# Five RMS norms around the end of the output projection: more of the squares' sum on VectorE, less on TensorE

## The chip, the cores and the metric

One core of one Trainium2 chip runs the whole kernel. The metric is the device time of one execution in microseconds (us), taken as the median of the runs. Engine names as in the profile: PE is TensorE (matmuls), PEld its weight load, DVE is VectorE, ACT is ScalarE, POOL is GpSimd, SP is the engine that issues the DMA transfers.

## The reference, cut to what matters

One layer of a decoder trunk, 1024 prompt tokens and 8 sample tokens, width 1024, all in fp32:

```python
def rms_norm(x, g):
    xf = x.astype(jnp.float32)
    r = xf * lax.rsqrt(jnp.mean(xf * xf, axis=-1, keepdims=True) + EPS)
    return (r * g.astype(jnp.float32)).astype(x.dtype)

def half_step_ffn(x, g_pre, g_post, w_gu, w_down):
    h = rms_norm(x, g_pre)
    gate, up = jnp.split(h @ w_gu, 2, axis=-1)
    y = (jax.nn.silu(gate) * up) @ w_down
    return x + 0.5 * rms_norm(y, g_post)

# per layer
xp = half_step_ffn(xp, ...)                                  # first FFN
att, ho = attention(...), hgrn2(...)                         # mixer
xp = xp + rms_norm(mixer_output(att, ho, ...), mix_post_g)   # output projection (1024 x 1024), its norm, the residual
xp = half_step_ffn(xp, ...)                                  # second FFN, with its own norm ahead
```

The change concerns the norm behind the output projection (`mix_post_g`) and the norm ahead of the second FFN: for each token the mean of 1024 squares.

## The kernel before

Activations lie with the 1024 features on partitions: 8 tiles (`KT`) of 128 features, and the 1032 tokens in three groups g of 344 (`GW`). So each activation of a group is 128 x 8 x 344. To keep fp32 accuracy, every dense product is split: ACT makes a rounded copy of weights and activations (`w_hi`, `x_hi`, type fp32r), DVE makes what is left (`w_lo`, `x_lo`, by a subtraction), and PE multiplies hi by hi, lo by hi and hi by lo. A unit is one output tile of one group: 8 x 3 matmuls of 344 columns.

**A norm.** ACT squares the group into one of two buffers (`square`: `sq_a` or `sq_b`, 8 tiles). DVE adds the upper half to the lower half (`fold`: 8 tiles become 4). PE multiplies what is left by a matrix of ones into one PSUM bank, and so sums over partitions and tiles at once (`norm_sum`; these matmuls are plain fp32, not the split kind, and the trace holds two records for each, so that x8 is four of them). ACT takes logarithm and exponential of it (`inverse`), which gives the reciprocal root `rms` or `rms_y`. A norm is named ("F", 1, g) where it belongs to the output projection's result y, and ("S", 2, g) where it belongs to the residual stream ahead of the second FFN. For eight other norms, named in `folded_twice`, DVE already adds a second time (4 tiles become 2) and PE has two tiles to sum. ("F", 1, 2) is done in halves by functions of its own (`last_fold`, `last_sum`) and is not touched.

**The order of the work.** Nothing is scheduled at run time: each engine has its instructions in an order written out by hand, and waits on semaphores. Around the change:

- PE: 24 output projection units k = 0..23 (`out_units`), group g = k // 8. The sums stand between them: ("F",1,0) behind unit 12, ("F",1,1) behind unit 18, ("S",2,0) behind unit 19. Then the halves of ("F",1,2), and between them and behind them the first units of the second FFN (`pair_unit`, by group and number o = 0 or 1: (0,0), (0,1), then ("S",2,1), then (1,0), (1,1), (2,0), then ("S",2,2), then (2,1)). Then `ffn`: six more opening units and the pair loop.
- DVE: for each unit k, `out_split(k)` (`w_lo` of the unit's weights) and `out_evac(k)` (PSUM to y). Among them stand the folds; `scaled(g)` (y times the reciprocal root), `added(g)` (y times gain, plus residual), `border_low(g)` (`x_lo` of the second FFN's input); and for group 2, behind the fold of ("S",2,1), `last_new` (the same scaling and adding in halves), `last_low`, and the fold of ("S",2,2). Behind that: `open_gate` and `open_up` (evictions of the FFN's first units), `normed`, and the sums and splits that the pair loop of the FFN needs.
- ACT: `out_split(k)` (`w_hi`), `square_y(g)`, `inverse`, `border_hi(g)` (`x_hi` for the second FFN from the new residual; waits for `added(g)`), `square_x(g)`.

The DVE part in the order written out, from the fold of ("F",1,1) on (set here on fewer lines):

```python
            fold(("F", 1, 1))
            out_split(19); out_evac(17); out_split(20)
            border_fold(0)
            out_evac(18); scaled(1); out_split(21); out_evac(19)
            added(1)
            out_split(22); out_evac(20); last_fold(0)
            out_split(23); out_evac(21); split_lo(G_FFN2, 0)
            border_low(1)
            out_evac(22); split_lo(G_FFN2 + 1, 1); out_evac(23)
            last_fold(1)
            border_fold(1)
```

ACT makes `w_hi` of unit 23 behind `border_hi(1)`, and `border_hi(1)` waits for `added(1)`. `Seq` (called `seq`) makes DVE wait for the end of its own instruction before the next.

Of the kernel before, what the change touches and what calls it, by code (L numbers as in the profile page):

```python
# [11 lines left out]
ALU = mybir.AluOpType  # L12
# [9 lines left out]
KT = D_MODEL // P  # L22
# [158 lines left out]
def build(nc, ins, outs):  # L181
    ctx = ExitStack()
    with ctx:
# [10 lines left out]
        def put(name, shape, dt, offset=None):  # L194
            size = (2 if dt == BF16 else 4) * int(np.prod(shape[1:]))
            if offset is None:
                offset = at[0]
                at[0] += (size + 31) // 32 * 32
            assert offset + size <= end, (name, offset + size - end)
            return nc.alloc_sbuf_tensor_at(name, shape, dt, offset=offset)  # L200
# [25 lines left out]
        sq_bufs = [put("sq_a", [P, KT, GW], F32), put("sq_b", [P, KT, GW], F32, h_at + 4 * GW * 4)]  # L226
# [68 lines left out]
        F, KG, HI, v_raw, HG = (FK[:, 0], FK[:, 3]), (FK[:, 1], FK[:, 4]), FK[:, 2], FK[:, 4], FK[:, 0:4]  # L295
# [54 lines left out]
        S = sems  # L350
# [6 lines left out]
        norm_no = {n: i for i, n in enumerate(norms)}  # L357
        sq_no = {n: 1 if n in (("S", 0, 1), ("F", 0, 1), ("S", 1, 1), ("S", 1, 0), ("S", 2, 0), ("S", 2, 1), ("S", 2, 2), ("F", 2, 1)) else 0 for n in norms}
        fold_no = {n: k for k, n in enumerate(n for n in norms if n[0] == "S")}
        y_fold_no = {n: k for k, n in enumerate(n for n in norms if n[0] == "F" and n[2] != (2 if n[1] == 1 else 0))}  # L360
# [4 lines left out]
        LAST_S1 = norm_no[("S", 1, 0)] + 1  # L365


        folded_twice = (("S", 0, 1), ("S", 0, 2), ("F", 0, 2), ("F", 0, 1), ("S", 1, 2), ("S", 1, 1), ("F", 2, 2), ("F", 2, 1))

        GAIN_F = {0: half_gain[:, 0, :], 1: vecs[:, V_GAIN["mix_post"]:V_GAIN["mix_post"] + 8], 2: half_gain[:, 1, :]}  # L370

# [246 lines left out]
        def _(pe):  # L618
# [13 lines left out]
            def norm_sum(n):  # L632
                i = norm_no[n]
                if n in fold_no:
                    pe.wait_ge(S["sq_folded"], fold_no[n] + 1)
                elif n in y_fold_no:
                    pe.wait_ge(S["y_folded"], y_fold_no[n] + 1)
                else:
                    pe.wait_ge(S["sq_done"], i + 1)
                tiles = KT // 4 if n in folded_twice else KT // 2 if n in fold_no or n in y_fold_no else KT  # L640
                if i >= 2:
                    pe.wait_ge(S["root_done"], i - 1)
                for m in range(tiles):
                    mm = nc.tensor.matmul(PS[:, sum_bank[n], :GW], ones[:], sq_bufs[sq_no[n]][:, m, :],  # L644
                                          start=(m == 0), stop=(m == tiles - 1))
                mm.then_inc(S["ss_done"], 1)

            def ffn(n0, u0, f, b):
# [118 lines left out]
                for k in range(BLOCKS):  # L767
                    block(k)
                    if k == 75:
                        norm_sum(("F", b, 2))  # L770
                    if k == 88:
                        norm_sum(("F", b, 1))
                    if b == 0 and k == 108:
                        pe.wait_ge(S["d_copied"], COPIED * f + N_LEAD)
                        norm_sum(("S", 1, 2))
                    if b == 0 and k == 116:
                        norm_sum(("S", 1, 1))
                    if k == 118:
                        half_sum(b, 0)
# [1031 lines left out]
        def _(dve):  # L1811
            seq = Seq(dve, S["dve_seq"])
# [10 lines left out]
                nc.vector.tensor_tensor(w_lo[s][:], raw[s][:], w_hi[s][:].bitcast(F32), ALU.subtract)\  # L1823
                    .then_inc(S["w_ready"], 1)

            def fold_again(n):

                q = sq_bufs[sq_no[n]]
                seq(nc.vector.tensor_tensor(q[:, 0:KT // 2], q[:, 0:KT // 2], q[:, KT // 2:], ALU.add))
                nc.vector.tensor_tensor(q[:, 0:KT // 4], q[:, 0:KT // 4], q[:, KT // 4:KT // 2], ALU.add)\  # L1830
                    .then_inc(S["y_folded" if n[0] == "F" else "sq_folded"], 1)

            def fold(n):
                if n in folded_twice:
                    dve.wait_ge(S["sq_done"], norm_no[n] + 1)
                    fold_again(n)
                    return
                q = sq_bufs[sq_no[n]]
                dve.wait_ge(S["sq_done"], norm_no[n] + 1)
                nc.vector.tensor_tensor(q[:, 0:KT // 2], q[:, 0:KT // 2], q[:, KT // 2:], ALU.add)\  # L1840
                    .then_inc(S["y_folded" if n[0] == "F" else "sq_folded"], 1)

            half_of = lambda a: slice(KT // 2 * a, KT // 2 * (a + 1))
# [53 lines left out]
            def ffn(n0, u0, f, b, slot_uses, hooks={}):  # L1897
# [272 lines left out]
                def fold_lead():  # L2170
# [3 lines left out]

                two = lambda a, b: lambda: (a(), b())
                behind = {2: lambda: h_sums(PAIR_STEPS, 1), 3: lambda: down_sums(PAIR_STEPS), 13: u2, 24: v, 30: c22, 35: c12, 37: lambda: fold(("F", b, 2)),
                          40: c21, 41: lambda: scaled_half(b, 2, 0), 42: lambda: scaled_half(b, 2, 1), 43: lambda: added_half(b, 2, 0),
                          44: lambda: fold(("F", b, 1)), 45: lambda: added_half(b, 2, 1),
                          49: lambda: scaled_half(b, 1, 0), 50: lambda: scaled_half(b, 1, 1), 51: lambda: added_half(b, 1, 0), 52: lambda: added_half(b, 1, 1),
                          59: fold_lead}  # L2180
                if b == 0:
                    behind.update({46: lambda: low_half(b, 2, 0, None), 47: lambda: low_half(b, 2, 1, S["x_split_lo"]),
                                   53: lambda: fold(("S", 1, 2)),
                                   54: lambda: low_half(b, 1, 0, None), 55: lambda: low_half(b, 1, 1, S["x_split_lo"]),
                                   57: lambda: fold(("S", 1, 1))})
# [390 lines left out]
                gained_low(1, g)  # L2576

            def border_fold(g):
                n = ("S", 2, g)
                q = sq_bufs[sq_no[n]]  # L2580
                dve.wait_ge(S["sq_done"], norm_no[n] + 1)
                nc.vector.tensor_tensor(q[:, 0:KT // 2], q[:, 0:KT // 2], q[:, KT // 2:], ALU.add).then_inc(S["sq_folded"], 1)

            def last_fold(a):
                q = sq_bufs[sq_no[("F", 1, 2)]]
# [107 lines left out]
            out_evac(17)  # L2693
            out_split(20)
            border_fold(0)
            out_evac(18)
            scaled(1)
# [12 lines left out]
            out_evac(23)  # L2710
            last_fold(1)
            border_fold(1)

            def last_halves():
# [3 lines left out]
            def last_lows():  # L2718
                last_low(0)
                last_low(1)  # L2720
                border_fold(2)
# [97 lines left out]
```

## Time and profile before

| | us |
|---|---|
| median of 3 runs | 1896.4 (1896.36 to 1897.34) |
| the profiled execution, its own time | 1896.69 |
| its span in the trace | 1894.9 |
| PE busy | 1869.7 (99% of the span) |
| DVE busy | 1369.5 (72%) |
| ACT busy | 802.9 (42%) |

The span is 1.8 us shorter than the execution's own time; that lies around it. Matmuls are pipelined and their ends are modelled: one of 344 columns is shown with 0.32 us and the next starts 0.16 us behind it. So a PE that is busy in the table need not be at its peak, and the starts of its instructions say more than its busy time. The same holds in part for DVE, whose instruction may start before the one ahead has ended.

### The profile page before, as it was taken

The numbers are of one execution on the slowest core, as the hardware profiler recorded it, in microseconds if no ns is written. First come the engines' busy times: TensorE is split into PE (matmuls) and PEld (weight loads), VectorE is DVE, ScalarE is ACT, GpSimd is POOL, SyncE is SP. The second block draws the span as 40 slices with busy tenths as digits, with TensorE's granted clock in tenths as the row PEclk, the third lists the DMA queues.
The fourth block names the chain that finished last, engine by engine and source line by source line (L and its number), as shares of the span: only waits on it lengthen the run. The fifth ranks groups of instructions, "written<-read, shape, count | busy, mean of one in ns | idle before, by whom it ended". The sixth has DMA issues, their size and how long they took to land. (4 is left out here: it accounts for less than half of the span.)

```text
span 1894.9 us, 36314 instructions
## 1 busy us (share of the span) xinstructions
PE 1869.7 (99%) x14337; PEld 1825.7 (96%) x14337; DVE 1369.5 (72%) x2127; ACT 802.9 (42%) x1278; POOL 35.0 (2%) x27
## 2 busy tenths in 40 slices
PE   9999999999999999999999999999999999999997
PEld 8999999999999999998998899999999999999997
DVE  7866767766656885578888678976776667755784
ACT  6422222323455673146565646532232223354553
POOL 0000000000000000000001100000000000000000
PEclk9999999999999999999999999999999999999999
DMA  5243334344798783210101465243334433599775
GB/s 190 101 160 130 138 132 144 122 155 159 257 294 262 221 264 117 56 49 25 36 25 35 141 242 171 83 158 136 144 122 152 150 138 132 172 310 292 226 240 181
DMA packets 115307, 296.60 MB, mean 157 GB/s; under 512 B 13136, under 2 KB 44760, under 8 KB 110328
## 3 DMA queue, kind: packets, MB, share of 16 engines
q1 hardware_dynamic: 115048, 294.93, 45.9%
q8 instruction: 84, 1.38, 0.3%
q14 instruction: 31, 0.25, 0.0%
q10 hardware_dynamic: 144, 0.03, 0.0%
HBM read 221.25 MB, written 73.00 MB: 155 GB/s over the span
## 5 line engine op out<-in xcount | busy, mean ns | idle before, releaser
L759 PE MATMUL PS<-x_hi,w_hi 128*128 128x344 f32 x960 | 309.3, 322 | 3.6 <-DVE w_lo L2122 3.6
L761 PE MATMUL PS<-x_hi,w_lo 128*128 128x344 f32 x960 | 306.7, 319 | 0.0
L760 PE MATMUL PS<-x_lo,w_hi 128*128 128x344 f32 x960 | 306.3, 319 | 0.0
L1290 ACT ACTIVATE silu_g<-silu_g 128x344 f32<-128x344 f32 x92 | 44.9, 491 | 458.8 <-DVE silu_g L2100 254.5
L663 PE MATMUL PS<-x_hi,w_hi 128*128 128x344 f32 x640 | 204.5, 320 | 0.0
L664 PE MATMUL PS<-x_lo,w_hi 128*128 128x344 f32 x640 | 204.1, 319 | 0.0
L665 PE MATMUL PS<-x_hi,w_lo 128*128 128x344 f32 x640 | 203.7, 318 | 0.0
L2129 DVE TENSOR_TENSOR x_lo<-t_raw,x_hi 128x688 fp32r<-128x688 f32 x120 | 104.1, 867 | 114.0 <-ACT x_hi L1398 113.4
L759 PEld LDWEIGHTS PS<-x_hi,w_hi 128*128 128x128 f32 x960 | 180.3, 188 | 5.6 <-DVE w_lo L2122 4.7
L760 PEld LDWEIGHTS PS<-x_lo,w_hi 128*128 128x128 f32 x960 | 180.2, 188 | 0.8
L761 PEld LDWEIGHTS PS<-x_hi,w_lo 128*128 128x128 f32 x960 | 180.2, 188 | 0.0
L1398 ACT ACTIVATE x_hi<-t_raw 128x688 fp32r<-128x688 f32 x120 | 92.8, 773 | 188.6 <-DMA t_raw<-spill_h 188.5
L1979 DVE TENSOR_TENSOR s_lo<-s_raw,s_hi 128x512 fp32r<-128x512 f32 x160 | 106.9, 689 | 82.0 <-ACT s_hi L1316 82.0
L1316 ACT ACTIVATE s_hi<-s_raw 128x512 fp32r<-128x512 f32 x160 | 100.5, 630 | 146.5 <-DVE s_raw L2086 138.8
L654 PE MATMUL PS<-x_sum,s_hi 128*128 128x344 f32 x480 | 154.1, 321 | 5.3 <-DVE s_lo L1979 4.9
L2122 DVE TENSOR_TENSOR w_lo<-raw,w_hi 128x1024 fp32r<-128x1024 f32 x120 | 146.9, 1224 | 14.0 <-ACT w_hi L1387 8.6
L654 PE MATMUL PS<-x_hi,w_hi 128*128 128x344 f32 x480 | 153.5, 320 | 0.9 <-ACT rms L1349 0.9
L655 PE MATMUL PS<-x_sum,s_hi 128*128 128x344 f32 x480 | 153.8, 320 | 0.0
L656 PE MATMUL PS<-x_sum,s_lo 128*128 128x344 f32 x480 | 153.7, 320 | 0.0
L656 PE MATMUL PS<-x_hi,w_lo 128*128 128x344 f32 x480 | 153.1, 319 | 0.0
L655 PE MATMUL PS<-x_lo,w_hi 128*128 128x344 f32 x480 | 152.7, 318 | 0.0
L1823 DVE TENSOR_TENSOR w_lo<-raw,w_hi 128x1024 fp32r<-128x1024 f32 x111 | 135.4, 1220 | 11.9 <-ACT w_hi L1253 7.0
(311 smaller groups left out, 4436.2 us busy)
## 6 DMA issues: line engine op xcount, KB each, us to landing
raw<-in_w_gu SPq DMA_DIRECT2D x88, 512.0 KB, 4.2
t_raw<-spill_h SPq DMA_DIRECT2D x238, 172.0 KB, 2.8
raw<-in_w_down SPq DMA_DIRECT2D x152, 256.0 KB, 3.6
d_raw<-in_w_down SPq DMA_DIRECT2D x44, 512.0 KB, 6.2
spill_s<-d_sum SPq DMA_DIRECT2D x22, 1024.0 KB, 5.2
raw<-spill_s SPq DMA_DIRECT2D x88, 256.0 KB, 4.4
spill_h<-T SPq DMA_DIRECT2D x22, 688.0 KB, 3.1
spill_h<-h_odd SPq DMA_DIRECT2D x22, 516.0 KB, 2.7
```

What stands on the lines that cost most here:

```text
L654: nc.tensor.matmul(PS[:, bank, :GW], wh[:, c], vh[:, k], start=(start and k == 0), stop=False, skip_group_check=not start)
L655: nc.tensor.matmul(PS[:, bank, :GW], wh[:, c], vl[:, k], start=False, stop=False, skip_group_check=not start)
L656: mm = nc.tensor.matmul(PS[:, bank, :GW], wl[:, c], vh[:, k], start=False, stop=(k == KT // 2 - 1), skip_group_check=not start)
L663: nc.tensor.matmul(PS[:, 7, :GW], wh, vh, start=(k == 0), stop=False)
L664: nc.tensor.matmul(PS[:, 7, :GW], wh, vl, start=False, stop=False)
L665: mm = nc.tensor.matmul(PS[:, 7, :GW], wl, vh, start=False, stop=(k == KT - 1))
L759: nc.tensor.matmul(PS[:, bank, :GW], hi[:, c], vh, start=opens, stop=False, skip_group_check=again)
L760: nc.tensor.matmul(PS[:, bank, :GW], hi[:, c], vl, start=False, stop=False, skip_group_check=again)
L761: mm = nc.tensor.matmul(PS[:, bank, :GW], lo[:, c], vh, start=False, stop=closes, skip_group_check=again)
L1823: nc.vector.tensor_tensor(w_lo[s][:], raw[s][:], w_hi[s][:].bitcast(F32), ALU.subtract)\
L1979: nc.vector.tensor_tensor(s_lo[k][:], s_raw[k][:], s_hi[k][:].bitcast(F32), ALU.subtract).then_inc(S["s_low"], 1)
L2122: return nc.vector.tensor_tensor(to[:], src[:], hi[:].bitcast(F32), ALU.subtract)
```

## The change

The choice of how often a norm's squares are added on DVE becomes a table. The norms ("S",0,0) and ("S",1,0) stay at one addition, the eight of the list stay at two. Five change: ("F",1,0), ("F",1,1) and ("S",2,2) get two additions instead of one (PE sums 2 tiles instead of 4), and ("S",2,0) and ("S",2,1) get three (PE sums 1 tile instead of 4).

```diff
-        folded_twice = (("S", 0, 1), ("S", 0, 2), ("F", 0, 2), ("F", 0, 1), ("S", 1, 2), ("S", 1, 1), ("F", 2, 2), ("F", 2, 1))
+        folds = {n: 1 for n in (*fold_no, *y_fold_no)}
+        folds.update({n: 2 for n in (("S", 0, 1), ("S", 0, 2), ("F", 0, 2), ("F", 0, 1), ("S", 1, 2), ("S", 1, 1), ("F", 2, 2), ("F", 2, 1))})
+        folds.update({("F", 1, 0): 2, ("F", 1, 1): 2, ("S", 2, 0): 3, ("S", 2, 1): 3, ("S", 2, 2): 2})
...
-                tiles = KT // 4 if n in folded_twice else KT // 2 if n in fold_no or n in y_fold_no else KT
+                tiles = KT >> folds.get(n, 0)
...
             def fold(n):
-                if n in folded_twice:
-                    dve.wait_ge(S["sq_done"], norm_no[n] + 1)
-                    fold_again(n)
-                    return
                 q = sq_bufs[sq_no[n]]
                 dve.wait_ge(S["sq_done"], norm_no[n] + 1)
-                nc.vector.tensor_tensor(q[:, 0:KT // 2], q[:, 0:KT // 2], q[:, KT // 2:], ALU.add)\
+                w = KT // 2
+                for _ in range(folds[n] - 1):
+                    seq(nc.vector.tensor_tensor(q[:, 0:w], q[:, 0:w], q[:, w:2 * w], ALU.add))
+                    w //= 2
+                nc.vector.tensor_tensor(q[:, 0:w], q[:, 0:w], q[:, w:2 * w], ALU.add)\
                     .then_inc(S["y_folded" if n[0] == "F" else "sq_folded"], 1)
...
             def border_fold(g):
-                n = ("S", 2, g)
-                q = sq_bufs[sq_no[n]]
-                dve.wait_ge(S["sq_done"], norm_no[n] + 1)
-                nc.vector.tensor_tensor(q[:, 0:KT // 2], q[:, 0:KT // 2], q[:, KT // 2:], ALU.add).then_inc(S["sq_folded"], 1)
+                fold(("S", 2, g))
```

## Rows read from the trace of the kernel before

**Rows 1.** The page: busy time by engine, share of the span, instructions.

```profile
PE 1869.7 (99%) x14337; PEld 1825.7 (96%) x14337; DVE 1369.5 (72%) x2127; ACT 802.9 (42%) x1278; POOL 35.0 (2%) x27
```

**Rows 2.** Busy time by stretch: length, PE, PEld, DVE, ACT, POOL, clock, DMA.

```profile
1150.00:1175.00 25.00, 25.00 (x148) 23.41 (x147) 22.37 (x29) 13.97 (x20) 0.00 (x0) 1.00 0.37 110
...
1205.00:1245.00 40.00, 39.52 (x250) 38.84 (x248) 37.98 (x50) 18.04 (x35) 0.00 (x0) 1.00 0.15 43
```

**Rows 3.** Timeline of PE around the sum of ("F",1,1): start, duration, instruction.

```profile
1153.22 0.32 PE L1075 MATMUL PS<-x_hi,w_lo 128*128 128x344 f32 x1
1153.37 2.48 PE L644 MATMUL PS<-sq_a,ones 128*128 128x344 f32 x8
...
1155.84 0.32 PE L1074 MATMUL PS<-x_lo,w_hi 128*128 128x344 f32 x1
```

**Rows 4.** Timeline of DVE: a fold and what follows; three small operations.

```profile
1150.72 1.58 DVE L1840 TENSOR_TENSOR sq_a<-sq_a 128x1376 f32<-128x1376 f32 x1
1152.22 1.22 DVE L2556 TENSOR_TENSOR w_lo<-raw,w_hi 128x1024 fp32r<-128x1024 f32 x1
...
1235.78 0.51 DVE L1987 TENSOR_TENSOR T<-h_even 128x344 f32<-128x344 f32 x1
1236.33 0.52 DVE L1991 TENSOR_TENSOR T<-h_odd,T 128x344 f32<-128x344 f32 x1
1236.76 0.51 DVE L1992 TENSOR_TENSOR T<-h_odd,h_even 128x344 f32<-128x344 f32 x1
```

**Rows 5.** One source line: second addition of the norms that have two.

```profile
L1830 DVE TENSOR_TENSOR sq_b<-sq_b x4: 874/875/877, 24.3 to 1814.2; 128x688 f32<-128x688 f32 x4
```

**Rows 6.** Timeline around the sum of ("F",1,0); in brackets idle time and releaser.

```profile
1126.03 1.58 DVE L1840 TENSOR_TENSOR sq_a<-sq_a 128x1376 f32<-128x1376 f32 x1
...
1128.23 2.47 PE L644 MATMUL PS<-sq_a,ones 128*128 128x344 f32 x8
...
1130.74 0.55 ACT L1268 ACTIVATE root<-PS,eps 128x344 f32<-128x344 f32 x1 [4.94 <-PE PS L644]
...
1131.85 3.02 DVE L2565 TENSOR_TENSOR y<-y,rms_y 128x2752 f32<-128x2752 f32 x1 [2.68 <-ACT rms_y L1273]
```

**Rows 7.** Timeline of DVE, ACT and PE from unit 18's eviction to unit 23.

```profile
1156.42 0.51 DVE L2560 COPY y<-PS 128x344 f32<-128x344 f32 x1
...
1156.98 3.02 DVE L2565 TENSOR_TENSOR y<-y,rms_y 128x2752 f32<-128x2752 f32 x1
...
1161.49 3.98 DVE L2571 SCALAR_TENSOR_TENSOR resid<-y,vecs,resid 128x344 f32<-128x344 f32 x8
...
1165.51 3.90 ACT L1278 ACTIVATE x_hi<-resid,vecs 128x344 fp32r<-128x344 f32 x8 [0.29 <-DVE resid L2571]
...
1169.31 1.04 ACT L1700 ACTIVATE w_hi<-raw 128x1024 fp32r<-128x1024 f32 x1
...
1170.38 1.22 DVE L2556 TENSOR_TENSOR w_lo<-raw,w_hi 128x1024 fp32r<-128x1024 f32 x1 [2.57 <-ACT w_hi L1700]
...
1173.05 0.32 PE L1073 MATMUL PS<-x_hi,w_hi 128*128 128x344 f32 x1
```

**Rows 8.** Timeline of DVE and PE, the border to the second FFN.

```profile
1182.86 1.59 DVE L2582 TENSOR_TENSOR sq_b<-sq_b 128x1376 f32<-128x1376 f32 x1 [1.52 <-ACT sq_b L1259]
...
1192.38 3.98 DVE L2612 SCALAR_TENSOR_TENSOR x_lo<-resid,vecs,x_hi 128x344 fp32r<-128x344 f32 x8
...
1197.46 1.59 DVE L2582 TENSOR_TENSOR sq_b<-sq_b 128x1376 f32<-128x1376 f32 x1 [1.10 <-ACT sq_b L1259]
...
1200.25 2.47 PE L644 MATMUL PS<-sq_b,ones 128*128 128x344 f32 x8
```

**Rows 9.** Timeline of DVE and PE, opening of the second FFN to its first pair.

```profile
1206.52 0.52 DVE L1922 TENSOR_TENSOR h_even<-PS,rms 128x344 f32<-128x344 f32 x1 [1.16 <-PE PS L807]
...
1245.55 0.69 DVE L1979 TENSOR_TENSOR s_lo<-s_raw,s_hi 128x512 fp32r<-128x512 f32 x1 [0.70 <-ACT s_hi L1316]
...
1246.50 0.40 PE L654 MATMUL PS<-x_sum,s_hi 128*128 128x344 f32 x1 [1.53 <-DVE s_lo L1979]
```

More of the change, by code:

```diff
@@ L1824, in split_lo @@
                     .then_inc(S["w_ready"], 1)
-            def fold_again(n):
-                q = sq_bufs[sq_no[n]]
-                seq(nc.vector.tensor_tensor(q[:, 0:KT // 2], q[:, 0:KT // 2], q[:, KT // 2:], ALU.add))
-                nc.vector.tensor_tensor(q[:, 0:KT // 4], q[:, 0:KT // 4], q[:, KT // 4:KT // 2], ALU.add)\
-                    .then_inc(S["y_folded" if n[0] == "F" else "sq_folded"], 1)
             def fold(n):
-                if n in folded_twice:
-                    dve.wait_ge(S["sq_done"], norm_no[n] + 1)
-                    fold_again(n)
-                    return
                 q = sq_bufs[sq_no[n]]
                 dve.wait_ge(S["sq_done"], norm_no[n] + 1)
-                nc.vector.tensor_tensor(q[:, 0:KT // 2], q[:, 0:KT // 2], q[:, KT // 2:], ALU.add)\
+                w = KT // 2
[3 more added lines that the diff above has]
+                nc.vector.tensor_tensor(q[:, 0:w], q[:, 0:w], q[:, w:2 * w], ALU.add)\
                     .then_inc(S["y_folded" if n[0] == "F" else "sq_folded"], 1)
@@ L2578, in border_fold @@
             def border_fold(g):
-                n = ("S", 2, g)
-                q = sq_bufs[sq_no[n]]
-                dve.wait_ge(S["sq_done"], norm_no[n] + 1)
-                nc.vector.tensor_tensor(q[:, 0:KT // 2], q[:, 0:KT // 2], q[:, KT // 2:], ALU.add).then_inc(S["sq_folded"], 1)
+                fold(("S", 2, g))
             def last_fold(a):
```

## The prediction, made before the run

> **What bounds the kernel now.** The page says PE: 99% busy, DVE 72% [rows 1]. That is a mean over stages, so I read next the busy time by stretch around the change. PE is busy throughout, but DVE is at 22.37 of 25 us around the last output units and at 37.98 of 40 us in the opening of the second FFN [rows 2]. Two engines are full there at once, and what the change takes from one it gives to the other. So the question is not how much PE saves, but which of the two each wait of the other ends at. For that I read the timelines of PE, DVE and ACT side by side [rows 6 to 9]: the reader is to look for the places where DVE stands idle (there it has slack) and for the releaser in brackets.
>
> **What PE saves.** Matmuls of a unit start 0.157 us apart. The last one ahead of the sum of four tiles starts at 1153.22, and the second one behind it at 1155.84; without the sum it would have started at 1153.22 + 2 x 0.157 = 1153.53. So four tiles cost 2.31 us, one tile 0.577 [rows 3]. The change removes 2 + 2 + 3 + 3 + 2 = 12 tiles: 6.92 us of PE.
>
> **What DVE pays.** A single fold occupies the queue for 1.50 us (1150.72 to 1152.22, though its own duration is 1.58: the next one overlaps the end). An operation that must wait for the one ahead starts 0.04 behind its end: 0.55 us from start to start for one of 0.51, against 0.43 where nothing is waited for [rows 4]. So with a second addition: 1.58 + 0.04, then 0.875 for 128x688 [rows 5] less the overlap of 0.08, together 2.41: **+0.91 us**. With a third: 1.62 + 0.91 + 0.43 = 2.96: **+1.46 us**; the add of one tile is not in the trace as a fold, I take 0.51 from the 128x344 adds [rows 4]. Over the five: 3 x 0.91 + 2 x 1.46 = 5.65 us. No DMA, and nothing on ACT or POOL, is added or moved.
>
> The trace shows 0.12 us more between two small operations where the second waits for the first [rows 4]. The Trainium skill (VectorE: DVE Perf Modes, section "The DRAIN you can't avoid") says that a semaphore between two operations costs nothing extra. By that the folds would add 0.88 and 1.39 us, and the final shift below would be 2.7 us instead of 2.9. The trace of this case disagrees with it on the small operations, and I go by the trace.
>
> **Where each piece lands.** I follow the shift of each engine against the times of before (minus is earlier).
>
> 1. ("F",1,0). The fold starts at 1126.03 and now ends at 1128.52 instead of 1127.61, but PE wants it at 1128.23 [rows 6]. PE starts 0.26 us behind what released it and its first matmul is 0.08 longer (s_lo ends at 1246.24, PE at 1246.50 with 0.40) [rows 9]. So the sum begins at 1128.78 and ends 0.55 + 0.08 - 1.15 = **-0.52** earlier. ACT waits for it, and DVE's scaling of group 0 waits for ACT (idle 2.68 us, which hides the 0.91) [rows 6]. So DVE and ACT gain 0.52 too. Bound: had PE not to wait, it would be -1.15.
> 2. ("F",1,1) and ("S",2,0). From the fold at 1150.72 up to the end of `added(1)` the view shows DVE without idle time (22.37 of 25 us busy to 1175, with 2.57 idle behind `added(1)` [rows 2, 7]), so both folds count in full: -0.52 + 0.91 + 1.46, less a gap of 0.13 ahead of 1156.98 (1156.42 + 0.43 = 1156.85) [rows 7]: **+1.72** for `scaled(1)` and `added(1)`. `border_hi(1)` on ACT waits for `added(1)` (idle 0.29), `w_hi` of unit 23 is behind it in ACT's queue, and DVE waited 2.57 us for just that before its split of unit 23 [rows 7]. So that DVE idle time doesn't absorb anything: what is late is its releaser. The split ends at 1170.38 + 1.22 + 1.72 = 1173.32, PE starts unit 23 at 1173.6 instead of 1173.05. PE has by then shed 7 tiles, 4.04 us, and stands 0.5 us later than before. Its gain has gone in waits for the fold of ("S",2,0) and for the splits of units 22 and 23.
> 3. ("S",2,1). The evictions, ACT's squares and this fold are all in the same chain (DVE waits 1.52 for ACT, which waits for DVE's last eviction): +1.72 at 1182.86. Its three additions make it **+3.18** for `last_new`, for ACT's `x_hi` and for `last_low` at 1192.38 [rows 8]. PE saves 3 tiles (1.73 us) behind unit (0,1). It began unit (2,0) one unit (24 x 0.157 = 3.76 us) ahead of 1200.25, at 1196.49; the first half of `last_low` was there at 1192.38 + 1.99 = 1194.4, a slack of 2.1 [rows 8]. With +3.18 that half comes at 1197.6, and PE waits for it.
> 4. ("S",2,2). The fold starts at 1197.46 + 3.18 = 1200.64 and ends at 1203.14; PE gets to the sum at 1203.4, 3.15 later than before, and is out of it at +2.1 after the two tiles saved. DVE is at 3.18 + 0.91 = **+4.09**.
> 5. Opening of the FFN. DVE's one slack: 1.16 us for PE at 1206.52 [rows 9]. PE, at +2.1, is there ahead of DVE, so DVE takes all of it: 4.09 - 1.16 = **+2.93**. From there to 1245.55 DVE is full [rows 2], the waits within are for ACT that itself waits for DVE, and PE's first pair of the loop waits 1.53 us for DVE's s_lo at 1246.50 [rows 9]. So PE leaves that point 2.93 us later than before. Behind it PE is the bound and nothing gives time back.
>
> **Sum.** The profiled execution took 1896.69, of which the span is 1894.9; 1896.69 + 2.93 = 1899.62. It stood 0.29 above the median of 1896.4, so I predict **1899.3**. The bounds of the unknown: 2.3 us if PE needn't wait in step 1; 4.1 us if step 5 absorbs nothing.
>
> **The rivals.**
>
> - *PE is the bound and the folds are covered.* The 12 tiles are all saved: 1896.4 - 6.9 = 1889.5. For it: 99% [rows 1] and no idle time of PE from 1150 to 1175, 25.00 of 25 us busy [rows 2]. Against it: the fold of ("F",1,0) already ends only 0.62 us ahead of PE [rows 6], and a gain of more than 0.5 to 2 us anywhere else is more than DVE's lead. It would need DVE's chain to gain as well, and only one of the five saves anything on that chain. The Trainium skill (Perfetto Trace Analysis, section "Identifying the Most-Contended Engine") says to take the engine with the highest occupancy and improve that first; by occupancy over the kernel that would be PE, and the time this rival's. Chance 0.04.
> - *The chain is looser at its link through ACT.* If `added(1)` doesn't set `w_hi` of unit 23 and with it the last evictions, the costs of ("F",1,1) and ("S",2,0) end there, and only 1.46 + 0.91 - 1.16 = 1.2 us are left: 1897.6. The 0.29 of idle time at 1165.51 speaks against it [rows 7]. Chance 0.12.
> - *Slower than the bound of what can be told.* If PE's end of unit (2,1) comes as late as DVE, the 1.16 us idle is not given back: +4.1 or a little more, 1900.5 and up to 1901. The point from which it begins is PE at over +2.9 there, where I have +2.1, so each of PE's new waits (units 22, 23, the halves of ("F",1,2), unit (2,0), the sum of ("S",2,2)) would have to cost more in its restart than the 0.34 us of [rows 9]. It has the same sign as the forecast, but beyond what counts as the same. Chance 0.17.
>
> A measurement of this kernel can tell 0.2% from no change: 3.8 us, so 1892.6 to 1900.2 is "same". My forecast is a small loss inside it, chance 0.67, with a range of its own of 1898.6 to 1900.3. Together: faster 0.05, same 0.76, slower 0.19. The range, from the looser chain's half to the slower rival: 1896.8 to 1901.0.
>
> **What would show it.** In the profile after: norm sums with x4, x4, x2, x2, x4 records; the sum of ("F",1,0) at about 1128.8; a wait of PE for `w_lo` ahead of units 22 and 23, and unit 23 at about 1173.6; the fold of ("S",2,1) at about 1184.6 and of ("S",2,2) at 1200.6; a PE wait for `x_lo` ahead of or in unit (2,0), and one for the last fold; no DVE idle time for PE at `h_even` (about 1209.4); the s_lo wait at about 1249.4. Wrong would be: unit 23 of the output projection ahead of 1171 (then the first rival), a fold at 1182.9 (then the second), or a granted clock below 1.00 [rows 2] behind one of PE's new waits, which would cost more than all of this.

## The result, and the profile after

The changed kernel takes 1900.13 us (median of 20 runs, 1898.44 to 1902.27) against 1897.35 us for the kernel before in its own 20 runs of the same comparison (1896.16 to 1899.66): a ratio of 1.0014, 95% interval 1.0008 to 1.0020. It is slower by 2.8 us, 0.14%, clear of noise but inside the 0.2% that the prediction called the same. The range held it; the predicted loss was 2.9 us. Single runs of one kernel lie up to 4 us apart here (1898.44 to 1902.27), so what follows goes by the traces, which give each start to 0.01 us.

The page of the profile after, and its busy time by stretch (the columns are those of [rows 1] and [rows 2]):

```profile
PE 1864.5 (98%) x14313; PEld 1820.6 (96%) x14313; DVE 1371.5 (72%) x2134; ACT 803.1 (42%) x1278; POOL 35.1 (2%) x27
```

```profile
1150.00:1175.00 25.00, 22.17 (x131) 20.43 (x131) 22.33 (x28) 13.14 (x20) 0.00 (x0) 1.00 0.32 93
1205.00:1245.00 40.00, 38.90 (x246) 38.31 (x245) 39.38 (x54) 19.58 (x35) 0.00 (x0) 1.00 0.12 36
```

PE has 24 records fewer (12 tiles) and is busy 5.2 us less, yet the span is 2.6 us longer, 1897.5 against 1894.9. From 1150 to 1175, where PE was busy throughout before, it now stands idle for 2.8 us. DVE, at 37.98 us of 40 in the opening of the second FFN before, is at 39.38.

The timeline of PE after, every place from 1127 to 1250 where it waited for more than 0.1 us, and the last matmul ahead of the first sum (start, duration, instruction, in brackets idle time and releaser):

```profile
1127.83 0.31 PE L1077 MATMUL PS<-x_hi,w_lo 128*128 128x344 f32 x1
...
1128.48 1.39 PE L646 MATMUL PS<-sq_a,ones 128*128 128x344 f32 x4 [0.34 <-issue]
...
1158.09 0.85 PE L646 MATMUL PS<-sq_b,ones 128*128 128x344 f32 x2 [0.45 <-DVE sq_b L1835]
...
1168.04 0.43 PE L1075 MATMUL PS<-x_hi,w_hi 128*128 128x344 f32 x1 [1.44 <-DVE w_lo L2551]
...
1173.04 0.42 PE L1075 MATMUL PS<-x_hi,w_hi 128*128 128x344 f32 x1 [0.94 <-DVE w_lo L2551]
...
1182.78 1.42 PE L1180 MATMUL PS<-sq_a,ones 128*128 128x344 f32 x4 [0.80 <-DVE sq_a L2583]
...
1197.38 0.39 PE L807 MATMUL PS<-x_hi,w_hi 128*128 128x344 f32 x1 [1.30 <-DVE x_lo L2604]
...
1202.84 1.42 PE L646 MATMUL PS<-sq_b,ones 128*128 128x344 f32 x4 [1.43 <-DVE sq_b L1835]
...
1208.72 0.42 PE L629 MATMUL PS<-x_hi,w_hi 128*128 128x344 f32 x1 [0.67 <-DVE w_lo L1825]
...
1248.92 0.40 PE L656 MATMUL PS<-x_sum,s_hi 128*128 128x344 f32 x1 [1.53 <-DVE s_lo L1974]
```

Before, none of these but the last was there (one more of 0.4 us, in the first pair, is in both traces and not shown). Seven are waits for DVE, in this order: the fold of ("S",2,0), the split of unit 22, that of unit 23, `last_fold`, `last_low` ahead of unit (2,0), the fold of ("S",2,2), the split ahead of the opening units. The one ahead of the first sum is put down to "issue" in its bracket, but the fold of ("F",1,0) ends 0.09 us before it (1127.51 + 0.88 = 1128.39, shown below), so it is a wait for DVE too. Together the eight are 7.37 us in the brackets. Each costs about 0.26 more than its bracket, for two reasons: the idle time is counted from the modelled end of 0.32 us though the next matmul could start at 0.157, and the matmul behind a wait is about 0.1 us longer (0.43 for 0.32). Together 7.37 + 8 x 0.26 = 9.5 us of waits against 6.92 us of sums removed: about 2.5 us lost, of the 2.67 that the traces show below; the rest was not traced.

The timeline of DVE after, at the places that answer to [rows 6 to 9]:

```profile
1125.89 1.59 DVE L1833 TENSOR_TENSOR sq_a<-sq_a 128x1376 f32<-128x1376 f32 x1
1127.51 0.88 DVE L1835 TENSOR_TENSOR sq_a<-sq_a 128x688 f32<-128x688 f32 x1
1128.30 0.51 DVE L2555 COPY y<-PS 128x344 f32<-128x344 f32 x1
...
1154.99 2.49 DVE L1833 TENSOR_TENSOR sq_b<-sq_b 128x1376 f32<-128x1376 f32 x2
1157.52 0.52 DVE L1835 TENSOR_TENSOR sq_b<-sq_b 128x344 f32<-128x344 f32 x1
1157.95 0.51 DVE L2555 COPY y<-PS 128x344 f32<-128x344 f32 x1
1158.38 3.01 DVE L2560 TENSOR_TENSOR y<-y,rms_y 128x2752 f32<-128x2752 f32 x1
...
1171.76 1.23 DVE L2551 TENSOR_TENSOR w_lo<-raw,w_hi 128x1024 fp32r<-128x1024 f32 x1 [2.57 <-ACT w_hi L1702]
...
1195.20 3.98 DVE L2604 SCALAR_TENSOR_TENSOR x_lo<-resid,vecs,x_hi 128x344 fp32r<-128x344 f32 x8
1200.29 1.59 DVE L1833 TENSOR_TENSOR sq_b<-sq_b 128x1376 f32<-128x1376 f32 x1 [1.10 <-ACT sq_b L1261]
...
1209.01 0.51 DVE L1917 TENSOR_TENSOR h_even<-PS,rms 128x344 f32<-128x344 f32 x1
```

Two additions occupy the queue from 1125.89 to 1128.30, 2.41 us, three from 1154.99 to 1157.95, 2.96 us. The 2.57 us of idle time ahead of unit 23's split are still there, moved along with their releaser. The 1.16 us ahead of h_even [rows 9] are gone.

**How shifts are measured below.** All traces are laid over one another at one point ahead of the change: the start of PE's last matmul before the sum of ("F",1,0) (1127.83 here, 1128.08 before). The shift of a place is its distance from that point less the same distance before. For the wait on s_lo: (1248.92 - 1127.83) - (1246.50 - 1128.08) = 121.09 - 118.42 = +2.67 us. The shifts are good to some 0.3 us and no better, although each start is given to 0.01: already ahead of the change, DVE's fold of ("F",1,0) starts 2.05 us before this point in the trace of before, 1.94 in that of the change and 1.74 to 2.04 in the others.

### The profile page after: what moved, and what is told of

It is laid out like the page before. It is cut to its first block and busy times, and to the rows that moved or that the text cites. A ratio compares the mean times of both kernels' runs of the same rounds, so it can differ in the third digit from the quotient of the medians.

```text
span 1897.5 us, 36273 instructions
## 1 busy us (share of the span) xinstructions
PE 1864.5 (98%) x14313; PEld 1820.6 (96%) x14313; DVE 1371.5 (72%) x2134; ACT 803.1 (42%) x1278; POOL 35.1 (2%) x27
## 3 DMA queue, kind: packets, MB, share of 16 engines
q8 instruction: 84, 1.38, 0.3%
```

## The experiments

One table for all. The diffs are against the changed kernel, cut to the lines that differ, except where another is named. The first five columns are shifts in us from the traces, against before: of DVE's `scaled(1)`, of its split of unit 23, of `last_low`, of the h_even of unit (2,1), and of PE's wait for s_lo in the first pair of the second FFN. Behind that wait the order of work is the same in all, and the rest of the span takes 648.1 to 648.8 us in nine of the ten traces (648.4 before); in that of experiment 2 it takes 650.1, for a wait far behind the five norms that the last section shows. Then the median less that of before in the same comparison, and the ratio with its 95% interval.

| kernel | scaled(1) | split 23 | last_low | h_even | s_lo wait | median | ratio |
|---|---|---|---|---|---|---|---|
| the change | +1.65 | +1.63 | +3.07 | +2.74 | +2.67 | +2.8 | 1.0014 (1.0008 to 1.0020) |
| 1, PE's part alone | -1.29 | -1.31 | -1.32 | -2.56 | -2.62 | -3.1 | 0.9985 (0.9975 to 0.9994) |
| 2, the two triples alone | +1.33 | +1.31 | +2.76 | +1.76 | +1.73 | +1.2 | 1.0007 (0.9997 to 1.0016) |
| 3, first and last alone | -0.64 | -0.64 | -0.64 | -0.96 | -1.03 | 0.0 | 0.9999 (0.9990 to 1.0008) |
| 4, doubles, one moved | -1.16 | -1.16 | -1.18 | -1.50 | -1.56 | -1.7 | 0.9994 (0.9985 to 1.0003) |
| 5, DVE's part alone | +2.85 | +2.83 | +4.27 | +4.15 | +4.15 | +4.6 | 1.0021 (1.0011 to 1.0030) |
| 6, the three doubles alone | +0.08 | +0.06 | +0.05 | -0.28 | -0.36 | -0.4 | 1.0000 (0.9991 to 1.0009) |
| 7, one moved, no additions | +0.01 | +0.01 | +0.45 | +1.06 | +1.07 | +1.1 | 1.0006 (0.9997 to 1.0015) |
| 8, as 4, once more | -1.21 | -1.23 | -1.24 | -1.56 | -1.64 | -1.6 | 0.9990 (0.9981 to 0.9999) |

The theory is the prediction's: the order of work makes DVE (with ACT's answers to it) the chain that decides from `scaled(1)` to the FFN's first pair, and PE's savings turn into waits. The main rival is that PE is the bound and each tile of 0.577 us counts.

**1. PE's part alone.** DVE adds once, as before; PE sums 2, 2, 1, 1 and 2 tiles. Half of the added squares are thus left out of three of the means, and three quarters of them out of the other two.

```diff
+        added_on_dve = {**folds, **{n: 1 for n in {("F", 1, 0): 2, ("F", 1, 1): 2, ("S", 2, 0): 3, ("S", 2, 1): 3, ("S", 2, 2): 2}}}
...
-                for _ in range(folds[n] - 1):
+                for _ in range(added_on_dve[n] - 1):
```

> TensorE sums 2, 2, 1, 1 and 2 tiles as in the change, VectorE adds only once as before (part of the squares is left out of the five means). Theory (VectorE's chain sets the end of this stretch): VectorE's chain gains only what the first norm gives, 1.15 us, and 0.1 to 0.2 of a gap, and the idle time of 1.24 us ahead of h_even; that is about -2.5 us against before, and TensorE waits ahead of units 22 and 23 in spite of the missing additions. Rival (TensorE is the bound, the 12 tiles are worth 6.9 us): -6.9 us.

Measured -2.62 by the trace and a ratio that excludes both no change and the rival's 6.9 us (0.9964). PE gives back 12 tiles and more than half of it goes in waits for DVE even though no addition was put there; the timeline of PE in this kernel:

```profile
1170.47 0.42 PE L1076 MATMUL PS<-x_hi,w_hi 128*128 128x344 f32 x1 [0.98 <-DVE w_lo L2552]
...
1180.21 1.42 PE L1181 MATMUL PS<-sq_a,ones 128*128 128x344 f32 x4 [0.80 <-DVE sq_a L2584]
...
1197.91 1.42 PE L647 MATMUL PS<-sq_b,ones 128*128 128x344 f32 x4 [0.55 <-DVE sq_b L1836]
...
1203.79 0.43 PE L630 MATMUL PS<-x_hi,w_hi 128*128 128x344 f32 x1 [0.67 <-DVE w_lo L1826]
```

So the ceiling of this idea, had DVE's additions been free, was 2.6 us and not 6.9. Of it 1.15 us is the first sum, on which DVE and ACT wait too, and 1.24 the idle time ahead of h_even.

**5. DVE's part alone.** All additions are made; PE still sums four tiles of each of the five buffers.

```diff
+        summed_on_pe = {**folds, **{n: 1 for n in {("F", 1, 0): 2, ("F", 1, 1): 2, ("S", 2, 0): 3, ("S", 2, 1): 3, ("S", 2, 2): 2}}}
...
-                tiles = KT >> folds.get(n, 0)
+                tiles = KT >> summed_on_pe.get(n, 0)
```

> VectorE makes all additions of the change, TensorE still sums four tiles in each of the five norms (so that some squares are counted twice in the five means). Theory: the first sum is late by 0.5 and takes VectorE's chain along; then +0.91 + 1.46 - 0.13, +1.46, +0.91, less 1.24 of idle time: +3.9 us against before at the first s_lo wait of the second FFN. Rival, TensorE is the bound and the folds are covered: 0. Rival, the two halves of the change are additive (with -2.6 for TensorE's part alone and +2.7 for both): +5.3.

Measured +4.15. Alone the two halves are worth -2.62 and +4.15, which adds up to +1.5; together they are +2.67. The theory's +3.9 is 0.25 short, the additive rival's +5.3 is 1.15 too high. The columns show where they fail to add up: from `last_low` to h_even PE's part alone gains 1.24 us (-1.32 to -2.56), since PE is there early and the idle time goes. DVE's part alone loses 1.03 less than its additions (4.27 + 0.91 = 5.18, measured 4.15), and the change 1.24 less (3.07 + 0.91 = 3.98, measured 2.74). The idle time ahead of h_even can be taken only once, so the loss of both together is higher by the 1.03 that the sum counts twice: 1.53 + 1.03 = 2.56, near the 2.67. Here h_even waits for PE for a moment (a start of 1211.45, 0.62 behind the gate eviction at 1210.83, where 0.43 is the pace). With four tiles in each sum PE is late enough to decide this start, by 0.2 us; of the 1.24 us of slack 1.03 is still given back, so the prediction's third rival, in which none is, doesn't hold here either.

**2. The two triples alone**, ("S",2,0) and ("S",2,1).

```diff
-        folds.update({("F", 1, 0): 2, ("F", 1, 1): 2, ("S", 2, 0): 3, ("S", 2, 1): 3, ("S", 2, 2): 2})
+        folds.update({("S", 2, 0): 3, ("S", 2, 1): 3})
```

> Only (S,2,0) and (S,2,1) are added three times; the other three stay at one addition. Theory: VectorE +1.46 - 0.13, then +1.46, less 1.24 of idle time: +1.6 us against before, with last_low at +2.8 and the last fold at +2.8. Rival that each norm of the five costs in the same measure: two of five of the change's 2.6, +1.0. Rival that TensorE is the bound: 6 tiles, -3.5 us.

Measured +1.73, with `last_low` at +2.76: the theory's numbers within 0.15 us. By the trace, six tiles less for PE made the kernel later; the ratio excludes the -3.5 us (0.9982), but neither no change nor the +1.0 of the other rival. The timeline of DVE shows how little of the slack ahead of h_even is left, 0.16 of 1.16:

```profile
1207.72 0.52 DVE L1917 TENSOR_TENSOR h_even<-PS,rms 128x344 f32<-128x344 f32 x1 [0.16 <-PE PS L809]
```

**6. The three doubles alone.**

```diff
+        folds.update({("F", 1, 0): 2, ("F", 1, 1): 2, ("S", 2, 2): 2})
```

> Only (F,1,0), (F,1,1) and (S,2,2) are added twice; the two (S,2,x) that had three additions stay at one. Theory: -0.6 + 0.91 - 0.13 at scaled(1) = +0.2, then +0.91 - 1.24: -0.1 us at the s_lo wait, no difference from before. Rival, costs in the same measure everywhere: +1.6. Rival, TensorE is the bound: 6 tiles, -3.5.

Measured -0.36 and a ratio of 1.0000, which excludes the -3.5 us; against the +1.6 only the trace speaks, since the interval reaches 1.0009. The difference of 3.0 us between this kernel and the change is what the second and third additions of ("S",2,0) and ("S",2,1), with PE's tiles of them, do on top: 2 x 1.46 for DVE.

**3. The first and the last alone.**

```diff
+        folds.update({("F", 1, 0): 2, ("S", 2, 2): 2})
```

> Only (F,1,0) and (S,2,2) are added twice; the three in between stay at one addition. Theory: the first norm's sum ends 0.7 us earlier and takes VectorE's chain along, the last one's second addition (+0.9) goes into the idle time of 1.24 ahead of h_even: -0.7 + 0.9 - 1.24 = -1.0 us, faster than before and than the change. Rival, costs in the same measure everywhere: +1.0 us. Rival, TensorE is the bound: -2.3 us.

Measured -1.03 by the trace; the median shows 0.0, with an interval of about 1.7 us to either side, which holds the theory's -1.0 and the rival's +1.0 alike and excludes only the -2.3. Between these two the trace speaks for the theory, the time does not. The first norm's double leads DVE's chain by 0.64, and the last one's +0.91 is taken by the idle time ahead of h_even: from -0.64 to -0.96.

**4 and 8. Doubles, and one norm moved.** ("S",2,1) stays at one addition; the fold of ("S",2,0) goes to where DVE waited for `w_hi` of unit 23, its sum behind unit 23, its root with it.

```diff
+        folds.update({("F", 1, 0): 2, ("F", 1, 1): 2, ("S", 2, 0): 2, ("S", 2, 2): 2})
...
             out_split(20)
-            border_fold(0)
             out_evac(18)
...
             last_fold(0)
+            border_fold(0)
             out_split(23)
...
-            out_units(19, 20)
-            norm_sum(("S", 2, 0))
-            out_units(20, OUT_TILES)
+            out_units(19, OUT_TILES)
+            norm_sum(("S", 2, 0))
...
-            inverse(("S", 2, 0))
             square_last(0)
...
             split_hi(1, 30, U_OUT + 23)
+            inverse(("S", 2, 0))
             square_last(1)
```

> (F,1,0), (F,1,1), (S,2,0) and (S,2,2) are added twice, (S,2,1) once; the fold of (S,2,0) stands behind last_fold(0), where VectorE waited 2.57 us for w_hi of unit 23, its sum behind unit 23 and its root ahead of the second half of squares on ScalarE. Theory: the chain loses 1.50 us of the fold of before and is -0.7 + 0.9 - 1.6 = -1.4 us at the split of unit 23, then +0.9 - 1.24: -1.7 us. Rival, TensorE is the bound: 8 tiles, -4.6 us. Rival, VectorE's total work counts wherever it stands (+3.6 us of additions against -4.6 us of TensorE): a change of less than 1 us.

> The moved kernel once more, for its time: -1.6 us against before by the trace, a ratio of 0.9992 with an interval that just leaves out 1 or doesn't.

Measured -1.56 and -1.64 by the traces, and in the second comparison a ratio of 0.9990 (0.9981 to 0.9999): the only version here with the whole computation whose interval lies below 1 (in the first comparison it reaches 1.0003). It is 4.3 us ahead of the change by the trace. The rival of -4.6 us (0.9976) is excluded; that total work decides (less than 1 us) is spoken against by both traces, though not by the intervals. What the move gives by itself under these additions was not run: the same four doubles without it would be +0.55 by an estimate from experiment 6 (-0.36 + 0.91), so the move would be worth some 2.1 us. The hole in DVE's timeline is filled, 0.15 us of 2.57 is left:

```profile
1166.29 1.59 DVE L1832 TENSOR_TENSOR sq_b<-sq_b 128x1376 f32<-128x1376 f32 x1
1167.92 0.87 DVE L1834 TENSOR_TENSOR sq_b<-sq_b 128x688 f32<-128x688 f32 x1
1168.95 1.23 DVE L2550 TENSOR_TENSOR w_lo<-raw,w_hi 128x1024 fp32r<-128x1024 f32 x1 [0.15 <-ACT w_hi L1701]
```

**7. The move without any addition.** All five norms at one addition, order as in 4 (the diff is against that kernel).

```diff
-        folds.update({("F", 1, 0): 2, ("F", 1, 1): 2, ("S", 2, 0): 2, ("S", 2, 2): 2})
+        folds.update({("F", 1, 0): 1})
```

> All five norms are added once as before; only the fold, the sum and the root of (S,2,0) stand where the moved kernel has them. Theory: scaled(1) then waits for the root of (F,1,1), which is no earlier than before, so that VectorE's 1.50 us become idle time ahead of it: at most -0.13, about 0 at the s_lo wait. Rival, VectorE's place in the chain is all that counts: -1.5 us.

Half a miss. The first step is as expected: `scaled(1)` stays where it was (+0.01) and the 1.50 us become idle time ahead of it. But the kernel loses 1.07 us. Timelines of DVE and PE:

```profile
1157.06 3.02 DVE L2559 TENSOR_TENSOR y<-y,rms_y 128x2752 f32<-128x2752 f32 x1 [1.57 <-ACT rms_y L1274]
...
1171.74 0.42 PE L1075 MATMUL PS<-x_hi,w_hi 128*128 128x344 f32 x1 [0.80 <-DVE w_lo L2550]
...
1207.65 0.52 DVE L1916 TENSOR_TENSOR h_even<-PS,rms 128x344 f32<-128x344 f32 x1 [1.78 <-PE PS L809]
```

I had looked at DVE only. In this kernel PE has all 20 tiles of the five norms to sum, and DVE waits 1.78 us for it at h_even, 0.62 more than before: PE is the bound at that place. The loss is that wait at unit 23 with its restart (0.80 + 0.26 = 1.06). The sum of four tiles was taken out from ahead of units 20 to 23 and put behind them. PE then reached unit 23 ahead of its split, waited 0.80, and had the 2.31 us still to do. A sum ahead of a wait fills it; behind it, it doesn't. In the kernel before PE already decides the start of h_even, where DVE waits 1.16 us for it, so that what PE loses ahead of it is lost in full; and of the two moved kernels only the one whose double additions take tiles from PE is faster.

## Why the prediction was right

It was right in its sign and mechanism, and in its size to 0.3 us, part of which is luck (below): +2.93 predicted, +2.67 in the trace, +2.8 in the medians. The predicted 1899.3 is 0.8 below the 1900.13 measured since it stood on the median of three runs, 1896.4; the twenty of the comparison gave 1897.35. Step by step, the first by these lines of PE in the change, around the sum of ("S",2,1):

```profile
1187.64 0.32 PE L809 MATMUL PS<-x_hi,w_lo 128*128 128x344 f32 x1
1187.80 0.74 PE L646 MATMUL PS<-sq_b,ones 128*128 128x344 f32 x2
...
1188.53 0.32 PE L808 MATMUL PS<-x_lo,w_hi 128*128 128x344 f32 x1
```

1. *PE's saving* (6.92 us). The 24 records are gone. Where PE doesn't wait for the sum, at the one tile of ("S",2,1), the price in the change is 1188.53 - 1187.64 - 2 x 0.157 = 0.58 us (0.577 predicted). That it doesn't count in full is shown by experiment 1.
2. *DVE's cost* (+0.91, +1.46). 2.41 and 2.96 us in the queue, less 1.50: exact. The third addition, bounded only by adds of other tiles, took 0.43 from start to start as assumed. The Trainium skill's sentence (VectorE: DVE Perf Modes, "The DRAIN you can't avoid"), by which the semaphores between the additions are free, would give 0.88 and 1.39 by the prediction's estimate; this trace goes against it by 0.03 to 0.07 us a fold.
3. *("F",1,0)*: the sum ends 0.58 earlier in the change (0.52 predicted). Experiment 1, where PE needn't wait, has its root 1.15 earlier, the bound as given.
4. *("F",1,1) and ("S",2,0)*: +1.72 predicted, +1.65 at `scaled(1)`, +1.63 at unit 23's split, with the 2.57 us of idle time not absorbing anything. PE starts unit 23 at +0.24, where +0.55 was predicted. Experiment 2 has 1.33 of its 1.46 at the same places. The looser-chain rival is excluded by that.
5. *("S",2,1)*: +3.18 at `last_low`, measured +3.07; PE waits 1.30 for it at unit (2,0).
6. *("S",2,2) and h_even*: PE begins the sum at +2.84 (3.15 predicted); h_even +2.93, measured +2.74. The slack is 1.24 and not 1.16: the bracket counts from the end of the operation ahead, and the next could start 0.08 before that. Experiments 2, 3 and 6 lose and gain by this slack as told.
7. *To the first pair*: +2.74 becomes +2.67, and the s_lo wait is 1.53 us in both traces.

What was mis-sized: the delay between DVE's end and PE's start. I took 0.26 us, from the s_lo wait. Behind the folds and splits it is 0.05 (the fold ends at 1158.04, PE starts at 1158.09) to 0.09 (1128.39 and 1128.48). At the first sum that is 0.17 us too much, and so the end of it should have come out 0.17 too late. It came out only 0.06 too late, because in this trace DVE's fold itself started 0.11 later against PE than in that of before, ahead of anything that the change touches: chance, and of the size by which traces of one order of work differ there (0.3 us). PE's new waits were forecast 0.3 us too late (steps 4 and 6), of which the same delay is 0.2; it doesn't count in the sum, because DVE and not PE decides behind them.

Two more of the prediction's sentences don't stand. It said that a measurement tells 0.2% from no change; twenty runs of each kernel told 0.14%, with an interval of 0.06% to either side. And a clock below 1.00 behind a wait would "cost more than all of this": the one that a trace shows, in experiment 2, cost about 1.5 us, less than the 2.9 forecast (last section).

On the rivals: that PE is the bound is excluded by experiments 1, 2 and the change itself. The Trainium skill's rule of the engine with the highest occupancy (Perfetto Trace Analysis, "Identifying the Most-Contended Engine"), which for TensorE judges the headroom by the weight loads and the flops and not by the matmuls' busy time, points at PE with 99% and at PEld with 96% alike; here PE's 12 tiles without any cost for DVE gave 2.6 us of 6.9, and experiment 5 shows a loss of 4.15 us from work on an engine at 72%. That h_even absorbs nothing happened neither in the change nor in experiment 5, where PE had all tiles to sum (+4.27 at `last_low` with 0.91 more to come, and +4.15 at h_even).

## What to carry to other kernels

Where two engines are full in the same stretch, as here, moving work from the one with the higher share to the other pays only if the receiver has idle time at that place, and only idle time that isn't itself waiting for something this work delays: 1.16 us ahead of h_even absorbed, 2.57 us ahead of unit 23's split didn't. Lay a fold into a wait whose releaser it can't delay; and leave the matmuls that fill the time ahead of a wait in front of it. Differences of a microsecond in a kernel of 1900 are read from distances inside the traces, not from medians.

## What was not expected of the hardware

PE starts 0.05 to 0.06 us behind DVE's end at six of its new waits (1158.09, 1168.04, 1173.04, 1182.78, 1202.84, 1208.72), but 0.26 us behind it at the s_lo wait, in the kernel before (1246.24 and 1246.50) and after (1248.66 and 1248.92) alike. Why the two differ wasn't tried. The granted clock from 1150 to 1175 stayed at 1.00, the level of 2.4 GHz, through the change's waits of up to 1.44 us.

One trace shows what the other level costs. In that of experiment 2, 419 us behind the s_lo wait, PE sat idle for 2.04 us, ran for 1.5 us as before, and then its matmuls started 0.29 us apart and not 0.157:

```profile
1666.24 0.42 PE L761 MATMUL PS<-x_hi,w_hi 128*128 128x344 f32 x1 [2.04 <-DVE w_lo L2117]
...
1667.77 0.45 PE L761 MATMUL PS<-x_hi,w_hi 128*128 128x344 f32 x1
...
1668.30 0.49 PE L763 MATMUL PS<-x_hi,w_lo 128*128 128x344 f32 x1
1668.58 0.49 PE L761 MATMUL PS<-x_hi,w_hi 128*128 128x344 f32 x1
...
1671.35 0.32 PE L762 MATMUL PS<-x_lo,w_hi 128*128 128x344 f32 x1
```

```profile
1669.00:1671.00 2.00, 2.00 (x9) 2.00 (x8) 0.23 (x1) 0.26 (x1) 0.00 (x0) 0.50 1.06 390
```

The granted clock of the second view, its third number from the end, is 0.50, the level of 1.2 GHz. Thirteen starts take 3.58 us (1667.77 to 1671.35) instead of 2.04, so about 1.5 us are lost. The wait is there in the trace of before too, with 1.38 us, and the clock of 1660 to 1680 is 1.00 there against 0.91 here. Why this wait is longer in one execution was not tried. It lies far from the five norms, and it is one reason why the time of an execution can say less of them than a distance inside the trace.
